# Normalising and transposing the input per row tile, halving the first weight piece, and moving two groups of transposes ahead in a two-block transformer kernel

## The reference, cut to what matters

```
h = concatenate([meta, x])                       # 272 rows of 1024
u = rmsnorm(h, mix_norm_w)
q, k, v, g_ret, lru_in, lru_gate, gate_a, gate_b = split(u @ w_in)
o = headnorm(chunk_retention(rotary(q), rotary(k), v))
y_ret = (silu(g_ret) * o) @ w_branch_ret
y_lru = (gelu(lru_gate) * rg_lru(conv(lru_in))) @ w_branch_lru
h = h + (sigmoid(gate_a) * y_ret + sigmoid(gate_b) * y_lru) @ w_out
g, up = split(rmsnorm(h, ffn_norm_w) @ w_ffn_in)
h = h + (silu(g) * up) @ w_ffn_out
```

## Time and profile before

| | |
|---|---|
| median of 3 runs | 1151.18 us (1149.7 to 1153.47) |
| profiled execution | 1144.04 us, of which the span is 1142.1 us |
| mean granted PE clock | 0.994 |
| PE busy | 1105.1 us (97%) |
| DVE busy | 731.5 us (64%) |
| ACT busy | 618.5 us (54%) |
| DMA | 215.07 MB, mean 188 GB/s |

### The profile page before, as it was taken

One profiled execution on the slowest core, in us unless ns is written; L12 is line 12 of the kernel. 1 busy time (PEld: TensorE's weight loads), 2 busy tenths in 40 slices (PEclk: granted clock), 3 DMA queues, 4 the chain that ended last, 5 costly groups with the idle time before them and its releaser, 6 DMA issues.

```text
span 1142.1 us, 17273 instructions
## 1 busy us (share of the span) xinstructions
PE 1105.1 (97%) x7128; PEld 980.8 (86%) x7128; DVE 731.5 (64%) x809; ACT 618.5 (54%) x724; POOL 64.8 (6%) x56
## 2 busy tenths in 40 slices
PE   8999999999999999999999999899999989899996
PEld 5998889999878999998897778699999858688885
DVE  6854665865555444546765568956453677988884
ACT  7543479662455344434645355854434357777772
POOL 0410200000100000000000000000011100000140
PEclk9999999999999999999999999999999999999998
DMA  8552254654554555554454434234555535899891
GB/s 305 171 187 88 75 189 164 238 174 159 207 206 156 188 188 196 195 194 147 147 190 143 148 111 148 78 144 148 197 185 182 187 148 181 332 355 350 323 347 63
DMA packets 30468, 215.07 MB, mean 188 GB/s; under 512 B 3377, under 2 KB 3505, under 8 KB 4929
## 3 DMA queue, kind: packets, MB, share of 16 engines
q1 hardware_dynamic: 28112, 199.61, 49.5%
q0 software_dynamic: 1872, 13.11, 3.0%
q10 hardware_dynamic: 416, 1.39, 0.3%
HBM read 213.04 MB, written 1.05 MB: 187 GB/s over the span
## 4 chain that ended last, share of the span: by engine, by line
PE 86%; DVE 8%; ACT 3%; issue 1%; DMA 0%; POOL 0%; DVEq 0%; SPq 0%; ACTq 0%; POOLq 0%
PE bank L526 26%; PE bank L528 26%; PE bank L527 26%; DVE wlo L1511 1%; ACT buf L1040 1%; PE bank L1014 1%; PE bank L587 1%; PE bank L939 1%; DVE wlo L1508 1%; ACT whi L1040 1%; PE bank L900 1%; PE bank L882 1%; DVE normedT_lo L1535 0%; PE bank L651 0%; DMA buf<-x_dram 0%
## 5 line engine op out<-in xcount | busy, mean ns | idle before, releaser
L1511 DVE TENSOR_TENSOR wlo<-raw,whi 128x2048 fp32r<-128x2048 f32 x139 | 320.7, 2312 | 213.6 <-ACT whi L1040 213.3
L1040 ACT ACTIVATE whi<-raw 128x2048 fp32r<-128x2048 f32 x168 | 320.8, 1915 | 140.4 <-PE bank L528 140.1
L1040 ACT ACTIVATE buf<-bank 128x512 f32<-128x512 f32 (+5 forms) x167 | 78.8, 510 | 192.1 <-PE bank L528 171.4
L526 PE MATMUL bank<-normedT_hi,whi 128*128 128x256 f32 x640 | 179.2, 280 | 3.3 <-DVE normedT_lo L1535 3.3
L527 PE MATMUL bank<-normedT_lo,whi 128*128 128x256 f32 x640 | 178.3, 279 | 0.0
L528 PE MATMUL bank<-normedT_hi,wlo 128*128 128x256 f32 x640 | 178.2, 278 | 0.0
L526 PE MATMUL bank<-xT_hi,whi 128*128 128x256 f32 (+1 forms) x448 | 127.8, 285 | 3.2 <-DVE xT_lo L1556 3.2
L528 PE MATMUL bank<-xT_hi,wlo 128*128 128x256 f32 (+1 forms) x448 | 127.6, 285 | 0.0
L527 PE MATMUL bank<-xT_lo,whi 128*128 128x256 f32 (+1 forms) x448 | 127.4, 284 | 0.0
L526 PEld LDWEIGHTS bank<-normedT_hi,whi 128*128 128x128 f32 x640 | 120.9, 189 | 4.5 <-issue 4.1
L528 PEld LDWEIGHTS bank<-normedT_hi,wlo 128*128 128x128 f32 x640 | 121.5, 190 | 0.0
(11 more groups left out here) (383 smaller groups left out, 2277.0 us busy)
## 6 DMA issues: line engine op xcount, KB each, us to landing
raw<-weights_dram SPq DMA_DIRECT2D x168, 1024.0 KB, 4.9
buf<-weights_dram SPq DMA_DIRECT2D x19, 1024.0 KB, 5.1
buf<-x_dram SPq DMA_DIRECT2D x2, 512.0 KB, 4.3
buf<-mem_dram ACTq DMA_DIRECT2D x1, 1024.0 KB, 9.7
out_dram<-buf SPq DMA_DIRECT2D x2, 512.0 KB, 3.0
buf<-final_w_dram POOLq DMA_DIRECT2D x1, 512.0 KB, 3.9
con<-consts_dram SPq DMA_DIRECT2D x1, 486.0 KB, 10.0
buf<-small_w_dram SPq DMA_DIRECT2D x1, 432.0 KB, 12.5
```

The source lines that it names most:

```text
L526: E.matmul(out_, lh, rh, start=start, stop=False)
L1040: return S.activation(out_, in_, func, **kw)
L1511: V.tensor_tensor(wlo[:, n % SLOTS, :], raw[:, n % SLOTS, :], whi[:, n % SLOTS, :].bitcast(f32), sub).then_inc(piece_split, 1)
```

## The change

The input's tokens are normalised tile by tile. PE transposes all blocks of row tile 0 into four banks, then those of row tile 1, then the meta rows, with short runs of spins between, and 19 spins instead of 28 at first. ACT does one root on an unused value at the very start. Piece 0 is rounded and split in two halves of 1024 columns, between which the transposed parts are taken; the first keys are multiplied over its first half for both banks, and then over its second. The meta rows are written by three DVE instructions for all eight blocks. The `params` transfer is cut in two: the small columns go ahead of piece 0, `wa2` to the end. `tr` is transposed before the last piece of `gate_b`, `tm` after `br_ret`; `th` between the two halves of `mem_k`. ACT and DVE follow in the same order. Banks are given out anew to match. Several semaphores of roots become one (`unit_rooted`), waited on by count.

```
 # bank order
-_fill("tx.0", "tx.1", "txm", "tx.2", "tx.3")
+_fill("tx.0", "tx.1", "tx.2", "tx.3", "txm")
...
+_fill(..., "gb.0", "gb.1", "gb.2")
+_fill(*_n("tr", 4), "gb.3", *_n("br", 4), *_n("tm", 4), *_n("bl", 4), *_n("out1", 2, 2))
+_next = 0
+_fill(*_n("mk.0", 2))
+_next = 4
+_fill(*_n("th", 4))
+_next = 2
+_fill(*_n("mk.1", 2))
 # SP
+            sp.dma_start(par[:, 0:PC["wa2"][0]], params[:, 0:PC["wa2"][0]]).then_inc(par_loaded, 16)
             sp.dma_start(raw[:, 0, :], weights[0]).then_inc(piece_loaded[0], 16)
-            sp.dma_start(par[:, :], params).then_inc(par_loaded, 16)
...
             sp.dma_start(SWR, small_w).then_inc(small_loaded, 16)
+            sp.dma_start(par[:, PC["wa2"][0]:], params[:, PC["wa2"][0]:]).then_inc(wa2_loaded, 16)
 # PE, start
-            spin(banks[7], 28)
+            spin(banks[7], 19)
             pe.wait_ge(ident_loaded, 16)
+            x_banks = [begin(f"tx.{j}") for j in range(4)]
+            for r in range(RT):
+                pe.wait_ge(normed["x"], r + 1)
+                for j in range(4):
+                    for kk in range(2):
+                        last = E.transpose(x_banks[j][...], XN[:, r, (2 * j + kk) * P:(2 * j + kk + 1) * P], ident)
+                    if r:
+                        last.then_inc(turned, 1)
+                spin(banks[7], 3)
+            turn("txm", ..., after=(normed["x"], RT + 1))
+            spin(banks[7], 6)
+            def first_keys():
+                outs = [begin(f"k.{c}") for c in range(2)]
+                moved(pe, "txm")
+                for half in range(2):
+                    if half == 0:
+                        pe.wait_ge(first_split, 1)
+                    else:
+                        pe.wait_ge(piece_split, 1)
+                    for c in range(2):
+                        for k in range(4 * half, 4 * half + 4):
+                            if c == 0:
+                                after_turn("tx")(k)
+                            last = product(outs[c][:, 0:TM], ...)
+                last.then_inc(pieces_used, 1)
 # PE, gate_b and mem_k
+            for j in range(3):
+                cols_product(PB["gate_b"] + j, XT, [f"gb.{j}"], first=META)
+            pe.wait_ge(o_ready, 1)
+            turn_rows("tr", O)
+            cols_product(PB["gate_b"] + 3, XT, ["gb.3"], first=META)
             for j in range(4):
-                cols_product(PB["gate_b"] + j, XT, [f"gb.{j}"], first=META)
+                cols_product(PB["br_ret"] + j, RTP, [f"br.{j}"], ready=None if j else after_turn("tr"))
             pe.wait_ge(normed["mem"], RT)
             turn_rows("tm", MR)
...
-            for c in range(2):
-                rows_product(PB["mem_k"] + 2 * c, MTP, _n(f"mk.{c}", 2), TT)
+            rows_product(PB["mem_k"], MTP, _n("mk.0", 2), TT)
             pe.wait_ge(normed["h"], RT)
             turn_rows("th", XN)
+            rows_product(PB["mem_k"] + 2, MTP, _n("mk.1", 2), TT)
 # ACT, start
+            A(warmed, zeros[:, 0:1], ACT.Sqrt)
             for r in range(RT):
                 act.wait_ge(x_loaded[r], 16)
                 A(XN[:, r, :], X[:, r, :], ACT.Square, accum_out=stat["x"][:, r:r + 1]).then_inc(squares, 1)
-            row_roots("x")
+                act.wait_ge(meansq, r + 1)
+                A(stat["x"][:, r:r + 1], stat["x"][:, r:r + 1], ACT.Sqrt).then_inc(rooted, 1)
...
+            turned_high("tx", XT[0][:, :, META:], W("mixw"), range(0, 1))
+            act.wait_ge(piece_loaded[0], 16)
+            A(whi[:, 0, 0:PW // 2], raw[:, 0, 0:PW // 2], ACT.Copy).then_inc(first_high, 1)
+            turned_high("tx", XT[0][:, :, META:], W("mixw"), range(1, 2))
+            A(whi[:, 0, PW // 2:], raw[:, 0, PW // 2:], ACT.Copy).then_inc(piece_high, 1)
             turned_high("tx", XT[0][:, :, META:], W("mixw"), range(2, 4))
 # DVE, start (x_norm: mean, wait for the root, reciprocal, scaled rows, for one tile)
+            for r in range(RT):
+                x_norm(r, P, X[:, r, :], XN[:, r, :])
+            x_norm(RT, META, XM, XM)
+            turned_low("tx", x_tokens, W("mixw"), range(0, 1))
+            dve.wait_ge(turned, turns["txm"])
+            chain(V.tensor_tensor(META_T, txm, bc(W("mixw"), META), mult))
+            chain(V.tensor_copy(XT[0][:, :, 0:META], META_T))
+            release(V.tensor_tensor(XT[1][:, :, 0:META], META_T, XT[0][:, :, 0:META].bitcast(f32), sub), "txm")
+            dve.wait_ge(first_high, 1)
+            V.tensor_tensor(wlo[:, 0, 0:PW // 2], ...).then_inc(first_split, 1)
+            turned_low("tx", x_tokens, W("mixw"), range(1, 2))
+            dve.wait_ge(first_split, 1)
+            dve.wait_ge(piece_high, 1)
+            V.tensor_tensor(wlo[:, 0, PW // 2:], ...).then_inc(piece_split, 1)
+            turned_low("tx", x_tokens, W("mixw"), range(2, 4))
             feed(dve, 2)
```

More of the change, by code:

```diff
@@ L410, in program @@
         stat = {n: tiny(3) for n in NORMS}
+        warmed = tiny(1)
         oss, mkss, ogss = tiny(RT, HR), tiny(RT, MH), tiny(RT, GH)
@@ L596, in _ @@
             pe.wait_ge(zeros_ready, 1)
[L597 removed]
+            spin(banks[7], 19)
             pe.wait_ge(ident_loaded, 16)
[L599 to L609 removed]
+            x_banks = [begin(f"tx.{j}") for j in range(4)]
[3 more added lines that the diff above has]
+                    for kk in range(2):
+                        last = E.transpose(x_banks[j][:, kk * T + r * P:kk * T + (r + 1) * P], XN[:, r, (2 * j + kk) * P:(2 * j + kk + 1) * P], ident)
+                    if r:
+                        last.then_inc(turned, 1)
+                spin(banks[7], 3)
+            turn("txm", [(k * META, XM[:, k * P:(k + 1) * P]) for k in range(KT)], after=(normed["x"], RT + 1))
+            spin(banks[7], 6)
+            def first_keys():
+                w = [part.rearrange("p (k c) -> p k c", k=KT) for part in (whi[:, 0, :], wlo[:, 0, :])]
+                outs = [begin(f"k.{c}") for c in range(2)]
[9 more added lines that the diff above has]
+                                after_turn("tx")(k)
+                            last = product(outs[c][:, 0:TM], both(w, ALL, k, slice(c * P, (c + 1) * P)), both(XT, ALL, k), k == 0, k == KT - 1)
+                last.then_inc(pieces_used, 1)
             def turn_v(j):
@@ L615, in turn_v @@
                     turn(f"tvm.{j // 2}", [(hh * P, VT[:, 4 * (j // 2) + hh, 0:META]) for hh in range(4)])
-            for p in range(4):
-                cols_product(PB["k"] + p, XT, [f"k.{2 * p}", f"k.{2 * p + 1}"], TM, ready=None if p else ready_x)
+            first_keys()
+            for p in range(1, 4):
+                cols_product(PB["k"] + p, XT, [f"k.{2 * p}", f"k.{2 * p + 1}"], TM)
             for p in range(4):
@@ L714, in down_step, with sums_free @@
                 last.then_inc(pieces_used, 1)
+            def sums_free():
+                for b in range(4):
+                    pe.wait_ge(evacuated[b], _ffn_uses[b])
             def hidden(base, steps, silu_done, act_done, hidden_low, ready=None):
@@ L731, in hidden @@
                 down_step(base + 3 * steps - 1, 0, steps - 1, hidden_low, steps, final=True)
-            th_banks = [BANKS[f"th.{j}"][0] for j in range(4)]
-            for b in range(8):
-                if b not in th_banks:
-                    pe.wait_ge(evacuated[b], _ffn_uses[b])
             hidden(PB["ffn"], FSTEPS, ffn_silu, ffn_act, low["ffn"], ready=after_turn("th"))
@@ L1159, in _ @@
             act.wait_ge(o_summed, 1)
-            A(oss, oss, ACT.Sqrt).then_inc(o_rooted, 1)
+            A(oss, oss, ACT.Sqrt).then_inc(unit_rooted, 1)
             for c in range(2):
@@ L1204, in _ @@
             for j in range(1, 4):
+                if j == 3:
+                    turned_high("tr", RTP[0])
                 full(act, PB["gate_b"] + j + 1)
                 release(A(GB[:, 2 * j:2 * j + 2, :], bank(f"gb.{j}")[:, :].rearrange("p (k t) -> p k t", k=2), ACT.Sigmoid), f"gb.{j}")
+            for j in range(4):
+                feed(act, PB["br_ret"] + j + 2)
             turned_high("tm", MTP[0], W("gmem"))
-            turned_high("tr", RTP[0])
             for j in range(4):
@@ L1551, in _, with x_norm @@
-            feed(dve, 0)
-            dve.wait_ge(par_loaded, 16)
-            turned_low("tx", tuple(part[:, :, META:] for part in XT), W("mixw"), range(0, 2))
-            dve.wait_ge(high["txm"], 1)
-            for k in range(KT):
-                last = V.scalar_tensor_tensor(XT[1][:, k, 0:META], bank("txm")[:, k * META:(k + 1) * META], W("mixw")[:, k:k + 1], XT[0][:, k, 0:META].bitcast(f32), mult, sub)
-            release(last, "txm")
-            turned_low("tx", tuple(part[:, :, META:] for part in XT), W("mixw"), range(2, 4))
+            def x_norm(at, rows_, src, dst):
+                s = stat["x"][0:rows_, at:at + 1]
+                dve.wait_ge(squares, squares_ahead["x"] + at + 1)
+                V.tensor_scalar(s, s, 1.0 / D, EPS, mult, add).then_inc(meansq, 1)
+                dve.wait_ge(rooted, at + 1)
```

(11 more changed lines are left out.)

109 lines of the change are left out of this document (47 added, 62 removed).

## The result

| | before | after |
|---|---|---|
| median of 6 runs | 1149.65 us (1145.45 to 1153.47) | 1137.56 us (1132.49 to 1144.58) |
| profiled execution | 1144.04 us | 1132.54 us |
| span of it | 1142.1 us | 1130.6 us |
| mean granted PE clock in it | 0.994 | 0.996 |

The ratio is 0.9887 [0.9844, 0.993]: faster by 12.1 us, where 8.1 was forecast.

The account below looks back on a forecast made before the run. PE's list of products was taken to bound the kernel, busy 97% of the span. Gains of 3.9, 1.87 and 3.31 less 0.95 sum to 8.1, taking 1151.18 to 1143.1 us; range 1139.5 to 1147.0.

Parts of the forecast that it names:

- part 1, the start: At the start: keys begin at 13.75 instead of 17.65, first piece ends at 19.9 instead of 23.78; gain 3.9 us.
- part 2, tr: Before br_ret: transposing tr ahead of gate_b's last piece removes the whole idle time; gain 1.87 us.
- the new wait: Before mem_k's first product: PE waits for DVE's addition to read out the bank of out1.1.0; loss 0.95 us.
- part 3, th: Before the feed-forward: transposing th between the halves of mem_k removes the whole idle time; gain 3.31 us.
- PE's clock: At the new start: twelve spins and 0.9 idle keep PE at its higher clock; no loss taken.
- DVE's queue: Rival at the start: piece 1 or 3 is split late and PE waits; gain 4.7 to 6.8, chance 0.17.
- the load ring: Rival at br_ret and br_lru: later splits delay loads and the ring starves; time 1154.6 us, chance 0.02.
- hidden bank wait: Rival before mem_k: DVE's addition overlaps PE's own start-up; gain 9.1, time 1142.1 us, chance 0.08.
- Clock falls over the new start: Rival at the start: products at half speed for 5 us lose 2.5; gain 5.6, time 1145.6, chance 0.05.
- Little: Rival: the start gains nothing, only parts 2 and 3 remain less a late split; gain under 3.4, chance 0.05.
- slower: Rival at br_ret and br_lru: the load ring starves through later splits; time 1154.6 us, chance 0.02.

Follow-up runs that it names:

- e4: The changed kernel with the retention transposes tr back behind gate_b, together with the memory's; 1140.15 us.
- e6: The changed kernel with banks read out earlier given to the first memory keys, th and second half moved along; 1133.19 us, ratio to before 0.9842.
- e1: The changed kernel executed again without any edit; 1140.94 us, ratio to before 0.989.
- e7: The changed kernel with th back behind all of mem_k and the old banks for mk and th; 1144.31 us.
- e9: The kernel of e6 with products of zeros put into five later idle times of PE; 1133.74 us, ratio to before 0.9841.
- e12: The changed kernel with one product of zeros between gate_b and br_ret; 1140.38 us.
- e2: The kernel before the change, executed again without any edit; 1152.68 us, median of 11.
- e3: The changed kernel with the old start taken back, tr and th staying ahead; 1143.29 us.
- e5: The kernel before the change with 14 products of zeros in each of PE's two long idle times; 1148.75 us, ratio to before 0.9975.
- e8: The changed kernel with piece 0 rounded and split as a whole, the keys waiting for all of it; 1140.06 us.
- e10: The changed kernel without the twelve products of zeros between the transposes at the start; 1134.37 us.
- e11: The changed kernel without ACT's early root on an unused value; 1143.17 us.

## Why the prediction was right or wrong

| term | forecast | measured |
|---|---|---|
| part 1, the start | 3.9 | 4.46 in the pair, 3.9 in the mean |
| part 2, tr | 1.87 | 2.92 (e4: 2.83) |
| the new wait | -0.95 | -1.25 (e6: -1.16) |
| part 3, th | 3.31 | 3.88 |
| sum | 8.1 | 10.0 in the pair, 9.5 with the start's mean |
| PE's clock | 0 | 2.2 to 2.6, what is left over |

**The mechanism was right at all four places.** Each idle time went, the new one came where the forecast had it, on the releaser that it named, at 0.98 idle for 0.95. DVE's queue and the load ring cost nothing: pieces 1 and 3 were split at 18.7 and 30.7, earlier than the 19.45 and 31.4 of the working, because DVE's list ran some 0.7 ahead of the working from meta on (11.87 for 12.55).

**Sizes.** The start was right within what it varies by. In this execution the spins ended sooner (7.1 for 19 against 7.6), meta's eight transposes took 0.6 for 0.9 and the meta operations 0.79 for 0.9, which, less a half split of 1.22 for 1.15, carries through to 13.19 for 13.75. In the seven profiles that have the new start unchanged (after, e1, e4, e6, e7, e9, e12) the keys begin at 13.19 to 13.93, 13.61 in the mean, and in the three with the old one (before, e2, e3) at 17.42 to 17.65, 17.54 in the mean: 3.9.

What varies is not the same in the two starts. The old one follows x's second tile, for which PE stood idle behind its spins: the tile's square starts at 5.84, 5.97, 6.08 and 6.33 (e2, e3, before, e5), and the keys come 11.6 behind it in each. In the new start the spins themselves are on the path: in all seven profiles the first transposes follow the last spin at once, at 7.12 to 7.90, and in six of them the keys come 6.0 to 6.1 behind that (6.3 in e4). The prediction said that the spins end before the wait for DVE, though by its own working they end at 7.6 and tile 0 is ready at 7.0. In after it made no difference, but in e1 the second tile is ready at 8.80 and transposed from 9.42 on. So fewer spins might gain up to some 0.6 in such executions; that was not tried.

For tr the idle time was taken for the whole price. The missing 0.9 is the pace of br_ret, 22.69 against 21.78, which no row of idle time shows. For th, 0.33 of the surplus lies in the feed-forward's first 24 products, 3.06 against 2.73 (also 3.06 in e5, where spins left 0.28 of the idle time, so it doesn't go with its length), and 0.24 around the change from one group to the next.

The new wait's stretch is 0.27 longer than its 0.98 of idle time. Of this 0.16 is how idle time is counted, from the end of the last product (310.47+0.40 in after), while without a wait the next one starts 0.23 behind its start (312.42 and 312.65 in e6); and 0.11 is no wait at all, since out1's first 24 products took 5.89 in after and in e6 and 5.78 in before.

**The step that failed is the paragraph on PE's clock.** It asked whether the new start could lose the clock, and answered from one profile: "The new start has twelve spins in that stretch and 0.9 idle, so I take no loss." That the old idle times could lose it was not asked, since the profile at hand had "3.18 of idleness" at full clock. Of the profiles with the old start unfilled (before, e2, e3) two have a half-clock stretch right behind the idle time (2.7 and 1.5 us), and of those with the old idle time before the feed-forward (before, e2, e7) two have one (2.5 in each). In the mean over these three and three profiles that is 1.4 and 1.7 us, 3.1 together. With spins in them the mean clock was higher and the mean time 3.1 us lower (e5), though with an interval that reaches no gain. So the gain over the runs, 12.1 in the first comparison and 11.7 in the second (1152.68-1140.94), is 9.5 of the parts and 2.2 to 2.6 that is left for the clock. That last figure is a difference, not a measurement; the 3.1 of the profiles and the 3.1 of e5 stand beside it.

**The level.** The forecast was 1143.1 and the result is 1137.56, 5.5 lower. 1.5 of that is before's own median, 1149.65 over six runs where three gave 1151.18. 1.4 is the sizes (9.5 for 8.1) and 2.6 what is left for the clock. The range reached below the forecast by a hidden bank wait and 2.5 of scatter, which holds none of the sizes and no clock gain; that is why it missed. The clock decided it: with 2.6 more the result would be 1140.2, inside the range; with the 1.4 of the sizes more 1139.0, or with the 1.5 of before's median more 1139.1, still outside.

**The rivals.** Clock falls over the new start: not in eight profiles with its spins and 0.83 of idle, but it does once with its spins and 1.89 (e8) and once without the twelve and 2.23 (e10), at 1.5 us each. DVE's queue: no. Bank wait hidden: no, it was dearer. Little, or slower: no.

## What to carry to other kernels

An idle time of PE costs its length and may cost more: the granted clock can fall in it or just behind it (1.5 to 2.7 us here, in some executions), and the products behind it may start later or run at another pace. So take the price of an idle time from several profiles, and read the granted clock beside each span before two spans are compared; two executions of one program differed by 8.7 us, most of it through that. When transposes are moved between products, give the next group the banks that were read out longest ago: that was worth 1.2 us here with no instruction saved. And when a start is made shorter, look again at what fills it: spins that once ended long before a wait may now be the wait.

## What the runs showed of the hardware that was not expected

- The same program ran with spans of 1130.6 and 1139.3, with the same idle times, and PE's clock at 0.996 and 0.987 in the mean. Five stretches at the lower level cost 1.6 to 2.6 us each in the second, 9.1 together, and a sixth, at 942, nothing; the slower outset cost 0.7, and groups that ran at a quicker pace gave about 1 back. Where stretches fall among small products (at 111 to 116, or at 124 to 132, in some executions) no run explains.
- 192 products of 128x256 take 21.8 or 22.7 us, about 113 or 118 ns each, at full granted clock; one product of zeros ahead of the group turns it (e12). Behind a half-clock stretch at a group's start the pace was the other one in e5 (br_ret 113.3 ns apart, 117.8 in before) and in e7 (the feed-forward's first group 117.8, 113.3 in before), but the same in e2 (113.3). The 256-column products of gate_b ran at 118 ns in the profiles before and after.
- In the cold start of ACT (e11) the table load took 1.28, and the root behind it started 0.01 after it; taking the load off the way to the first root brought the keys forward by 0.3 to 1.0.
